# Four calls moved inside the head-pair loop of a sparse-attention phase

## What is computed

```
q = rmsnorm(heads(q, 16), q_g)            # 16 heads of 64
q_nope, q_rope = q, partial_rope(q)
s_c = q_nope . k_cmp * scale ; o_c = masked_softmax(s_c) . v_cmp      # compressed keys
s_s = q_rope . k_sel * scale ; o_s = masked_softmax(s_s) . v_sel      # selected blocks
s_w = q_rope . k_win * scale ; o_w = masked_softmax(s_w) . v_win      # window
o   = gate0 * o_c + gate1 * o_s + gate2 * o_w
return o @ w_out
```

## Time and profile before

| what | value |
| --- | --- |
| median of 3 executions | 2896.3 us (2894.27 to 2896.97) |
| profiled execution | 2894.27 us, its span 2892.5 us |
| busy over the span: PE, DVE, ACT, POOL | 2776.4, 1645.3, 1196.6, 151.1 us |
| mean granted TensorE clock | 0.984 of full speed |
| the head-pair loop | from about 2242 to 2468 us of the span |

### The profile page before, as it was taken

The page is one execution under the profiler, slowest core; times in us unless marked ns, Lnnn a source line. Parts: engine busy times, 40 slices in busy tenths (PEclk is TensorE's granted clock), DMA queues, the critical chain, the costliest instruction groups (busy, mean ns, idle before and its releaser), DMA issues.

```text
span 2892.5 us, 34273 instructions
## 1 busy us (share of the span) xinstructions
PE 2776.4 (96%) x11831; PEld 2095.8 (72%) x11831; DVE 1645.3 (57%) x2264; ACT 1196.6 (41%) x1929; POOL 151.1 (5%) x141
## 2 busy tenths in 40 slices
PE   8999998999989988999989989999997999999999
PEld 6777776888867656888857557888875555788887
DVE  4444426776254755777249955554364777555532
ACT  4333324444243544444236654333244666433321
POOL 0000000000000000000005700000000222000000
PEclk9999999999999999999999999999998999999999
DMA  4222232333322112333322213333333000233322
GB/s 144 75 78 73 73 94 69 98 92 93 95 76 81 52 44 66 101 90 94 92 73 59 59 51 88 94 94 92 96 95 98 15 16 23 73 95 94 93 88 94
DMA packets 419614, 229.32 MB, mean 79 GB/s; under 512 B 7939, under 2 KB 411468, under 8 KB 419404
## 3 DMA queue, kind: packets, MB, share of 16 engines
q1 hardware_dynamic: 418172, 225.18, 26.7%
q10 hardware_dynamic: 1360, 3.08, 0.3%
HBM read 226.14 MB, written 2.10 MB: 79 GB/s over the span
## 4 chain that ended last, share of the span: by engine, by line
PE 83%; DVE 9%; ACT 5%; issue 2%; DMA 1%; POOL 1%; DVEq 0%; ACTq 0%; POOLq 0%; SPq 0%
PE lin L729 21%; PE lin L730 21%; PE lin L731 21%; DVE con_a L2384 2%; PE stat L745 1%; DVE w_lo L1937 1%; PE lin L1042 1%; PE att L874 1%; PE att L839 1%; PE att L838 1%; PE att L837 1%; PE att L1003 1%; ACT w_hi L1351 1%; PE lin L1065 1%; PE trp L1020 1%
## 5 line engine op out<-in xcount | busy, mean ns | idle before, releaser
L1937 DVE TENSOR_TENSOR w_lo<-raw,w_hi 128x1024 fp32r<-128x1024 f32 x427 | 527.7, 1236 | 648.3 <-ACT w_hi L1351 634.4
L1351 ACT ACTIVATE w_hi<-raw 128x1024 fp32r<-128x1024 f32 x427 | 452.3, 1059 | 774.4 <-PE lin L731 684.1
L729 PE MATMUL lin<-xh,w_hi 128*128 128x512 f32 x1856 | 741.5, 399 | 4.4 <-DVE w_lo L1937 3.9
L730 PE MATMUL lin<-xl,w_hi 128*128 128x512 f32 x1856 | 733.4, 395 | 0.0
L731 PE MATMUL lin<-xh,w_lo 128*128 128x512 f32 x1856 | 733.3, 395 | 0.0
L729 PEld LDWEIGHTS lin<-xh,w_hi 128*128 128x128 f32 x1856 | 348.2, 188 | 97.2 <-issue 12.0
L730 PEld LDWEIGHTS lin<-xl,w_hi 128*128 128x128 f32 x1856 | 348.3, 188 | 86.7 <-issue 3.4
L731 PEld LDWEIGHTS lin<-xh,w_lo 128*128 128x128 f32 x1856 | 348.1, 188 | 85.0
L730 PE MATMUL lin<-ffn_lo,w_hi 128*128 128x512 f32 x704 | 279.1, 396 | 0.0
L729 PE MATMUL lin<-ffn_hi,w_hi 128*128 128x512 f32 x704 | 279.1, 396 | 0.0
L731 PE MATMUL lin<-ffn_hi,w_lo 128*128 128x512 f32 x704 | 279.1, 396 | 0.0
(11 more groups left out here) (366 smaller groups left out, 3809.9 us busy)
## 6 DMA issues: line engine op xcount, KB each, us to landing
raw<-in_ffn_w_up SPq DMA_DIRECT2D x176, 512.0 KB, 3.8
raw<-in_ffn_w_down SPq DMA_DIRECT2D x64, 512.0 KB, 3.8
raw<-in_a_w_in SPq DMA_DIRECT2D x48, 512.0 KB, 3.8
raw<-in_ffn_w_down SPq DMA_DIRECT2D x32, 384.0 KB, 3.3
raw<-in_conv_w_pw SPq DMA_DIRECT2D x24, 512.0 KB, 4.0
raw<-in_nsa_w_in SPq DMA_DIRECT2D x21, 512.0 KB, 3.8
raw<-in_a_w_out SPq DMA_DIRECT2D x16, 512.0 KB, 3.8
raw<-in_w_kv SPq DMA_DIRECT2D x16, 512.0 KB, 3.9
```

Source lines behind the costliest of these rows:

```text
L729: pe.matmul(bank, w_hi[s][:, k, :], h, start=start and k == 0, stop=False)
L730: pe.matmul(bank, w_hi[s][:, k, :], l, start=False, stop=False)
L1351: act.activation(w_hi[s][:, :, :], raw[s][:, :, :], ACT.Copy).then_inc(hi_done[s], 1)
L1937: dve.tensor_tensor(w_lo[s][:, :, :], raw[s][:, :, :], w_hi[s][:, :, :].bitcast(F32), ALU.subtract).then_inc(lo_done[s], 1)
```

## The change

On DVE, `raw_q(p + 1)` goes ahead of `weights(n)` at i = 2, and the weight split `split_next()` goes from i = 0 of the next pair, behind `top(2)`, to i = 6 of the pair itself, behind `top(8)` and ahead of `weights(7)`. On PE, `head_sums` goes from i = 3 (between `scores(5)` and `turn(3)`) to the end of i = 2 (behind `turn(2)`, ahead of `scores(5)`), and `partners` goes from i = 4 (behind `scores(6)`) to the end of i = 3 (behind `turn_compressed`, ahead of `scores(6)`). No operation is added, dropped or resized; ACT, POOL and SP programs are the same. Seven pairs (0 to 6) have these calls; the last pair prepares no queries.

```diff
@@ PE, loop over i
                         if i == 0 and p:
                             weigh(p - 1, 1, before)
-                        if i == 4 and not last_pair:
-                            partners(lin[ub][:, :], qn[:, 1 - p % 2, :], 5 + p + 1)
                         if i == 4:
                             weigh_compressed(p, own[0])
                             weigh(p, 0, own[0])
-                        if i == 3 and not last_pair:
-                            head_sums(lin[ub])
                         turn(n)
                         if i == 3:
                             turn_compressed(p, *own)
+                            if not last_pair:
+                                partners(lin[ub][:, :], qn[:, 1 - p % 2, :], 5 + p + 1)
+                        if i == 2 and not last_pair:
+                            head_sums(lin[ub])
@@ DVE, loop over i
-                        weights(n)
                         if i == 2 and not last_pair:
                             b = raw_q(p + 1)
+                        weights(n)
                         if i == 0:
                             compressed_weights(p)
                         if n + 2 < 8 * (NH // 2):
                             top(n + 2)
-                        if i == 0 and p:
-                            split_next()
                         if i == 1 and p:
                             low_out(p - 1, before)
                         if not last_pair:
@@
                                 rotated_q(p + 1, b)
+                            if i == 6:
+                                split_next()
                             if i == 7:
                                 compressed_top(p + 1)
```

## The result

The changed kernel takes 2909.38 us (median of 6, 2904.03 to 2911.1) against 2893.27 for the kernel before in the same series: a ratio of 1.0051, 95% interval 1.004 to 1.0062, so 16.1 us slower. In a second series it was 2909.97 against 2894.61, ratio 1.0054 (1.004 to 1.0068). The forecast was 15.4 us slower, from 2896.3 to 2911.7.

What follows compares the result with a forecast made beforehand. PE, busy 96% of the span, was taken as the bound, with 1.17 us idle a pair. Losses of 7.4 + 8.0 = 15.4 us on the 2896.3 median gave 2911.7; likeliest range 2909 to 2915.5, with rivals 2903 to 2924.

Steps and rivals of the forecast that it cites:

- likeliest case: Whole kernel: both losses are paid over seven pairs, 12.8 to 19.0 us slower, 2909 to 2915.5; chance 0.62.
- Both terms: Over seven pairs: PE's two moved calls cost 7.4 us, the moved weight split 8.0 us.
- `raw_q` costs nothing: At i = 2: `raw_q` gains nothing, and the lateness of `turn(2)` hides under the wait for ACT's square: 0.
- The prediction's aside: At i = 2: without the wait for the square as cover, late `turn(2)` would cost 0.3 to 0.4 us a pair.
- `head_sums` and `partners`, forecast 1.05 a pair: At i = 2 to 4: PE waits for square and scaled queries without scores as cover; 1.05 us a pair, bounds 0.85 to 1.5.
- The split, forecast 1.15 a pair: At i = 6 to 7: the split delays `weights(7)`, for which PE waits; 1.15 us a pair, bounds 0.98 and 1.22.
- The lower bound, 0.98: Split ahead of `weights(7)`: 1.13 us to the next reciprocal, less the 0.15 PE already waited.
- One term is hidden: Either the split or PE's moved calls find cover; only 7.4 or 8.0 us remains, 2903.7 or 2904.3; chance 0.12.
- Nothing changes: Whole kernel: each delay meets a PE wait of the same size; 2896.3 us, within 0.2%; chance 0.08.
- faster: Query chain: earlier `head_sums` and `partners` close PE's gaps; at best 8.2 us gained, 2888; chance 0.07.
- The clock falls: Around i = 2 to 4: PE's added idle lowers the clock, 1.7 us a pair, 12 us in all, 2924; chance 0.11.
- the prediction's own sign: Middle of the loop: windows with clocks under 1.00 would show the forecast wrong.

Runs made afterwards that it cites:

- experiment 4: Only `raw_q` moved ahead of `weights(2)`, against the kernel before the change: ratio 1.0003 (0.9994 to 1.0012), pair 28.23 us.
- experiment 6: Only the weight split moved, to i = 7 behind `weights(7)` and `top(9)`, against the kernel before: ratio 1.001 (1.0001 to 1.0019), pair 28.22 us.

## Why the prediction was right, step by step

**Size and sign.** 15.4 us were forecast and 15.4 to 16.1 measured, inside the likeliest case's own range of 12.8 to 19.0. The way and the mechanism are right, but the match to the microsecond is luck. Both terms were too large: 0.83 a pair lies just under the lower bound of the first, 0.85, and 0.98 on that of the second. The pairs bring 12.8, and a lower mean clock and the scatter of medians, neither of them in the sum, add the rest.

**`raw_q` costs nothing.** Right: it waits for the dense result, `turn(2)` is 0.25 later behind the dense matmul, and the wait for the square takes that up. Alone it changes no pair (experiment 4). The prediction's aside, that without this cover it would cost 0.3 to 0.4 us a pair, is wrong: the wait for `exps(3)` covers it just as well.

**`head_sums` and `partners`, forecast 1.05 a pair.** The mechanism is right: an idle 0.5 for the square, an idle 0.5 for the queries (0.6 was forecast), no idle left ahead of `normed_q`, and nothing given back from i = 5 on (`scores(7)` is 0.83 late, as much as the pair). `weigh_compressed` is 0.94 late. The term was too large by 0.2, as the pair grows by 0.83 alone. Half of that is the score tile, which I took at 0.85 to 0.92 and which takes 0.75 from its start to the next (2317.07 to 2317.82). The other half is given back at once: `weigh_compressed` takes 0.95 to the next start behind the scores, and took 1.06 (2316.01 to 2317.07) behind `partners`. The sum closes: 0.18 that `partners` is late, 0.75 for the scores, less 0.11, is 0.82.

**The split, forecast 1.15 a pair.** Right in place and sign; 0.98 measured. I took the split's step to the next reciprocal, 1.13, and a little more as what is put in, and overlooked that the reciprocal already waited 0.13 for `exps(7)`. The lower bound, 0.98, turned out to be the value, but for another reason: it took off the 0.15 that PE already waited for `weights(7)`, and that wait saves nothing, since a later `weights(7)` adds to it in full. That nothing is won at i = 0, nor in the last pair, was right: line 2289 now idles 3.2 us there (1.97 before), and PE gains nothing by it.

**The rivals.** "One term is hidden": out, both are seen alone. "Nothing changes" and "faster": out. The inverse root hardly moves:

```profile
2312.75 0.71 ACT L1365 ACTIVATE log_ms<-lin,eps 128x512 f32<-128x512 f32 x1
...
2313.58 0.74 ACT L1365 ACTIVATE log_ms<-lin,eps 128x512 f32<-128x512 f32 x1
```

The first is the kernel before, the second the changed one: 4.56 and 4.52 us behind the last dense matmul, so the earlier `head_sums` is worth 0.04 there, and `normed_q` then waits for `top(5)` anyway. "The clock falls": the steady pairs of the first profile all ran at 1.00, so it doesn't hold as priced, a fall in each pair. But it isn't absent: one pair in seven of one profiled execution lost 1.46 us behind PE's new wait, near the 1.7 of the rival. By the prediction's own sign, a clock under 1.00 in the middle of the loop, that pair speaks against the forecast. It should have been a small term of the sum and not a case of its own. The Trainium skill ("TensorE: Matmul & The Clock Gate", section "HAM oscillation — how this bites in real kernels") tells of the clock lost again at every turn of a loop; here the two traces of the changed kernel show it behind one wait of 1.08 us for `weights(7)` out of fourteen.

**What stays open.** How often the clock falls in the loop is known from few executions: in the fourteen traces kept of all kernels, six of them with longer waits in the loop than before, the steady pairs run at 1.00 but for that one. The mean clocks of the others cover all phases, and can't say whether their 0.0007 was lost in this loop.

## What to carry to other kernels

Calls that wait are placed by what is queued behind them: an instruction moved up in an in-order queue, ahead of work that could have filled its wait, loses that work's length (0.65 us a pair for `partners`, whose cover was a score tile of 0.75), and two such moves under one chain lose it once. Work that waits for nothing, as the split, costs its own length where the bound engine waits for what stands behind it (0.98), and nothing where that engine has other work (28.22 against 28.23 us with the split at i = 7). Find the stretch where the bound engine waits for others, and bring to it work that depends on nothing; here one dense chunk at i = 6 and one at i = 2 made 1.04 us a pair of a visible idle time of 1.17. When a move is cheap in the steady loop, look at the last turn, where the cover may be missing.

## What was not expected of the hardware

PE waits more than the idle time in its rows says. The chunk at i = 6 is 0.70 us of matmuls, put where PE was idle for 0.22 and 0.15 by the rows, and 0.66 of it vanished. The rows of that kernel show where:

```profile
2317.64 0.47 PE L1066 MATMUL lin<-xh,w_hi 128*128 128x512 f32 x1
...
2318.41 0.49 PE L1020 MATMUL trp<-const,n_e 128*128 128x128 f32 x3
...
2319.16 0.70 PE L1003 MATMUL att<-k_all,qr 64*128 64x256 f32 x4
```

`turn(6)`, six transposes, takes 0.75 from its start to the next here, and took 1.00 in the kernel before, at i = 6 of the pair in the earlier trace rows:

```profile
2322.78 0.87 POOL L706 TENSOR_SCALAR n_e<-n_e,n_sm,gates 128x384 f32<-128x384 f32 x1 [3.17 <-DVE n_sm L2301]
...
2323.25 0.55 PE L1020 MATMUL trp<-const,n_e 128*128 128x128 f32 x3 [0.21 <-DVE n_e L2304]
...
2323.70 0.55 PE L1020 MATMUL stat<-const,n_e 128*128 128x128 f32 x3
...
2324.25 0.70 PE L1003 MATMUL att<-k_all,qr 64*128 64x256 f32 x4
```

Two more waits stand in there, and no row names them. POOL's scaling of the second head ends at 2323.65, and the second three transposes start 0.05 behind it. The last instruction of `exps(7)` ends at 2324.20, and `scores(9)` starts 0.05 behind that. It is so in each of the seven pairs. With the chunk ahead of `turn(6)` both are over in time: POOL is done 0.30 before the second half starts, and `exps(7)` 0.18 before the scores. That fits the whole 0.25. How it divides is not shown in full: in the last pair of experiment 6, where `exps(3)` had long ended and POOL alone was late, six transposes took 0.93. PE's busy records cover such waits: their ends are modelled, as the page of the profile says, and the three transposes have 0.55 here and 0.49 there. In the same way a busy time per pair read from the rows (27.05 of 28.23) makes PE look fuller than it is, and the 1.17 us of idle time in a pair, which the prediction takes for all there is to win, is too small a number.
